# A state-space stage reordered on TensorE, VectorE and ScalarE

## The reference

```python
acs = cumsum(a)                                        # per chunk of 128 tokens
decay = exp(where(lower, acs_i - acs_j, -inf))
cb = einsum('cign,cjgn->cijg', Cm, Bm)
y = einsum('cijgh,cjghp->cighp', cb * decay, xdt)      # inside a chunk
states = einsum('cjgn,cjghp->cghpn', Bm, xdt * exp(acs_last - acs))
h_next = h * exp(acs_last) + states                    # across chunks
y += einsum('cign,cghpn->cighp', Cm, h_in) * exp(acs)
...
ssm = rms_norm((D * xs + y_forward + y_backward) * silu(z), gnorm_g)
```

## Time and profile before

| what | us |
|---|---|
| three runs | 1209.51, 1210.97, 1211.55 |
| their median | 1210.97 |
| the profiled execution | 1211.39 |
| span of its core | 1209.1 |
| busy: TensorE, VectorE, ScalarE | 1160.4, 698.0, 499.5 |
| mean granted clock of TensorE | 0.997 of 2.4 GHz |

### The profile page before, as it was taken

The page is one execution under the profiler, slowest core; times in us unless marked ns, Lnnn a source line. Parts: engine busy times, 40 slices in busy tenths (PEclk is TensorE's granted clock), DMA queues, the critical chain, the costliest instruction groups (busy, mean ns, idle before and its releaser), DMA issues.

```text
span 1209.1 us, 18264 instructions
## 1 busy us (share of the span) xinstructions
PE 1160.4 (96%) x7450; PEld 948.5 (78%) x7450; DVE 698.0 (58%) x1176; ACT 499.5 (41%) x756; POOL 8.5 (1%) x16
## 2 busy tenths in 40 slices
PE   4999999999999999999999999999889998999998
PEld 3777776687688888888887767898455897999998
DVE  3499998853542334423333378986769546456544
ACT  4343235652443332222222333366358635554442
POOL 0100000000000000000000000000000000000000
PEclk9999999999999999999999999999999999999999
DMA  9745345016553222333124563344021157546532
GB/s 358 257 140 202 138 157 202 1 62 218 180 168 105 87 73 84 130 113 104 50 73 143 192 210 105 106 138 140 1 93 48 53 180 256 176 146 215 194 116 93
DMA packets 121933, 166.49 MB, mean 138 GB/s; under 512 B 4509, under 2 KB 112391, under 8 KB 117639
## 3 DMA queue, kind: packets, MB, share of 16 engines
q1 hardware_dynamic: 121430, 164.99, 40.9%
q10 hardware_dynamic: 433, 0.51, 0.2%
HBM read 164.44 MB, written 1.05 MB: 137 GB/s over the span
## 4 chain that ended last, share of the span: by engine, by line
PE 75%; DVE 18%; ACT 4%; DMA 2%; issue 2%; SPq 0%; ACTq 0%; POOL 0%; DVEq 0%
PE acc L1929 20%; PE acc L1930 20%; PE acc L1931 20%; DVE Y L1258 6%; DVE w_lo L555 2%; PE acc L1991 1%; PE pmod L1868 1%; PE acc L1993 1%; PE acc L1992 1%; PE p L1816 1%; PE acc L1816 1%; DMA xin<-in_ctx 1%; DVE sm L1341 1%; PE acc L2562 1%; PE p L2149 1%
## 5 line engine op out<-in xcount | busy, mean ns | idle before, releaser
L555 DVE TENSOR_TENSOR w_lo<-raw,w_hi 128x1024 fp32r<-128x1024 f32 x234 | 259.0, 1148 | 247.7 <-ACT w_hi L545 247.3
L545 ACT ACTIVATE w_hi<-raw 128x1024 fp32r<-128x1024 f32 (+1 forms) x236 | 221.5, 987 | 436.3 <-PE acc L1931 407.0
L1929 PE MATMUL acc<-Hhi,w_hi 128*128 128x512 f32 (+1 forms) x976 | 334.4, 343 | 6.5 <-POOL ptap L627 4.5
L1930 PE MATMUL acc<-Hlo,w_hi 128*128 128x512 f32 (+1 forms) x976 | 331.7, 340 | 0.0
L1931 PE MATMUL acc<-Hhi,w_lo 128*128 128x512 f32 (+1 forms) x976 | 331.7, 340 | 0.0
L1929 PEld LDWEIGHTS acc<-Hhi,w_hi 128*128 128x128 f32 x976 | 185.9, 190 | 31.6 <-issue 8.5
L1931 PEld LDWEIGHTS acc<-Hhi,w_lo 128*128 128x128 f32 x976 | 185.8, 190 | 20.4
L1930 PEld LDWEIGHTS acc<-Hlo,w_hi 128*128 128x128 f32 x976 | 186.0, 191 | 19.8
L1929 PE MATMUL acc<-hid_hi,w_hi 128*128 128x512 f32 (+1 forms) x448 | 157.2, 351 | 0.0
L1930 PE MATMUL acc<-hid_lo,w_hi 128*128 128x512 f32 (+1 forms) x448 | 155.8, 348 | 0.0
L1931 PE MATMUL acc<-hid_hi,w_lo 128*128 128x512 f32 (+1 forms) x448 | 155.8, 348 | 0.0
(11 more groups left out here) (351 smaller groups left out, 1362.6 us busy)
## 6 DMA issues: line engine op xcount, KB each, us to landing
raw<-in_mod_w SPq DMA_DIRECT2D x48, 1024.0 KB, 5.3
raw<-in_ffn_w_in SPq DMA_DIRECT2D x44, 1024.0 KB, 5.1
raw<-in_od_w_in SPq DMA_DIRECT2D x15, 1024.0 KB, 5.3
raw<-in_ffn_w_out SPq DMA_DIRECT2D x16, 768.0 KB, 4.2
raw<-in_ev_w_in SPq DMA_DIRECT2D x10, 1024.0 KB, 7.5
raw<-in_ffn_w_out SPq DMA_DIRECT2D x16, 640.0 KB, 3.9
raw<-in_od_w_out SPq DMA_DIRECT2D x8, 1024.0 KB, 6.1
raw<-in_ev_w_out SPq DMA_DIRECT2D x8, 768.0 KB, 6.1
```

The source lines that it names most:

```text
L545: nc.scalar.activation(w_hi[:, w % 2, c0:c1], raw[:, r % RAW_SLOTS, c0:c1], ACT.Copy)\
L555: nc.vector.tensor_tensor(w_lo[:, w % 2, c0:c1], raw[:, r % RAW_SLOTS, c0:c1], w_hi[:, w % 2, c0:c1].bitcast(F32), ALU.subtract).then_inc( ...
L1929: mm(outs[m], hi[:, j, cols], xh, start=(first and j == 0), stop=False)
L1930: mm(outs[m], hi[:, j, cols], xl, start=False, stop=False)
```

## The change

TensorE: decays 0 and 1 go ahead of state products 0 to 2; the wait for `CB` moves behind products 3 and 4; decays 4 and 5 are issued after across 3, so that the decays run two steps ahead; each group b is `intra` twice, two decays, `inter`, two decays, and the sum of the group before, which also waits for `yg_ready` (its bank is the one that gating reads first). Modulation units 0 and 1 of the last group go ahead of the last sum, units 2 and 3 to the place where 0 and 1 were, and none is left in the pair loop's rounds; the first waits for decay 15 instead of the final root. VectorE: `masked(0)` behind `xw(2)`; `xw(4)` ahead of `join(1)`; `join` multiplies into `from_w`, ahead of its wait for the product, and adds from there; each chunk's addition right after its second `scaled`; both masked decays of a group ahead of the gating of the group before; the reciprocal of `qsc` ahead of the last gating. ScalarE: a dummy exponential first; decays 0 and 1 ahead of the state copies, two copies per state ahead of decays 2 and 3; squares after q = 9 and 13; the root of `qsc` after decay 15, then the squares of groups 2 and 3; the dummy root is gone.

```diff
@@ -971,14 +971,29 @@
                     f = 2 * (n - 12)
                     A(Z[:, f:f + 2, :], acc[:, lo:lo + 2, 0:LAT], ACT.Silu).then_inc(read_act, 1)
 
-            act.wait_ge(s("qsc_copied"), 1)
-            A(qsc[:, 0:LT, :], qsc[:, 0:LT, :], ACT.Sqrt, scale=1.0 / C_HD, bias=epsc[:, 0:1]).then_inc(s("qsc_root"), 1)
+            step(A(sm[:, 0, 7:8], epsc[:, 0:1], ACT.Exp))
             act.wait_ge(s("cb_mm"), 1)
             A(CB, pmod[:, :].rearrange("p (n i) -> p n i", n=4), ACT.Copy).then_inc(s("cb_ready"), 1)
-            for k in range(4):
-                act.wait_ge(s("xw_used"), (2, 2, 5, 5)[k])
-                A(state[:, k // 2 * 2, k % 2, :], acc[:, k % 2, :], ACT.Copy)\
-                    .then_inc(s("state_act"), 1)
+
+            def decay(q):
+
+                act.wait_ge(s("seg_mm"), q + 1)
+                if q >= 4:
+                    act.wait_ge(s("intra_mm"), q // 2 - 1)
+                A(seg[:, q % 4, :], RB(q), ACT.Exp).then_inc(s("decay_ready"), 1)
+
+            def state_copy(k):
+
+                act.wait_ge(s("xw_used"), 3 * k + 2)
+                for g in range(2):
+                    A(state[:, 2 * k, g, :], acc[:, g, :], ACT.Copy).then_inc(s("state_act"), 1)
+
+            decay(0)
+            decay(1)
+            state_copy(0)
+            state_copy(1)
+            decay(2)
+            decay(3)
 
             def square_y(b):
 
@@ -989,14 +1004,13 @@
                     A(ysq[:, f % 2, :], XC[:, f, 0:LAT], ACT.Square).then_inc(s("ysq_ready"), 1)
 
 
-            for q in range(16):
-                act.wait_ge(s("seg_mm"), q + 1)
-                if q >= 4:
-                    act.wait_ge(s("intra_mm"), q // 2 - 1)
-                A(seg[:, q % 4, :], RB(q), ACT.Exp).then_inc(s("decay_ready"), 1)
-                if q % 4 == 3 and q > 3:
-                    square_y(q // 4 - 1)
-            A(sm[:, 0, 7:8], epsc[:, 0:1], ACT.Sqrt)
+            for q in range(4, 16):
+                decay(q)
+                if q in (9, 13):
+                    square_y(q // 4 - 2)
+            act.wait_ge(s("qsc_copied"), 1)
+            A(qsc[:, 0:LT, :], qsc[:, 0:LT, :], ACT.Sqrt, scale=1.0 / C_HD, bias=epsc[:, 0:1]).then_inc(s("qsc_root"), 1)
+            square_y(2)
             square_y(3)
 
             act.wait_ge(s("ssy_mm"), KD)
@@ -1664,13 +1678,13 @@
             def join(k, used):
 
                 dve.wait_ge(s("state_act"), 2 * k)
-                dve.wait_ge(s("xw_used"), used)
-                to, frm = state[:, 2 * k - 1, :, :], state[:, 2 * k - 2, :, :]
-                step(V_.tensor_tensor(to.rearrange("p g (h n) -> p (g h) n", n=S_HD),
+                kept, frm = from_w[:, k - 1, :], state[:, 2 * k - 2, :, :]
+                step(V_.tensor_tensor(kept.rearrange("p (h n) -> p h n", n=S_HD),
                                       frm.rearrange("p g (h n) -> p (g h) n", n=S_HD),
                                       EX[:, 7 + k, :].unsqueeze(2).to_broadcast([P, S_HEADS, S_HD]), ALU.mult))
+                dve.wait_ge(s("xw_used"), used)
                 for g in range(2):
-                    ins = V_.tensor_tensor(state[:, 2 * k - 1, g, :], state[:, 2 * k - 1, g, :],
+                    ins = V_.tensor_tensor(state[:, 2 * k - 1, g, :], kept[:, g * 512:(g + 1) * 512],
                                            acc[:, 2 + g, :], ALU.add)
                 ins.then_inc(s("state_dve"), 1)
 
@@ -1693,24 +1707,25 @@
                                  CB[:, 2 * c + b // 2, :].unsqueeze(1).to_broadcast([P, 4, P]), ALU.mult)\
                     .then_inc(s("m_ready"), 1)
 
+            def both_ways(c, used):
+
+                dve.wait_ge(s("scaled_ready"), used)
+                V_.tensor_tensor(SCALED[c, 0], SCALED[c, 0], SCALED[c, 1], ALU.add).then_inc(s("across_ready"), 1)
+
             xw(2)
+            masked(0)
             xw(3)
+            xw(4)
             join(1, 3)
-            xw(4)
             xw(5)
-            masked(0)
             join(2, 6)
             scaled(0)
             scaled(1)
             masked(1)
             scaled(2)
+            both_ways(1, 3)
             scaled(3)
-            dve.wait_ge(s("scaled_ready"), 4)
-            for c in range(LT):
-                V_.tensor_tensor(SCALED[c, 0], SCALED[c, 0], SCALED[c, 1], ALU.add).then_inc(s("across_ready"), 1)
-            dve.wait_ge(s("qsc_root"), 2)
-            step(V_.reciprocal(qsc[:, 0:LT, :], qsc[:, 0:LT, :]))
-            step(V_.tensor_scalar(qsc[:, 0:LT, :], qsc[:, 0:LT, :], C_HD ** -0.5, None, ALU.mult))
+            both_ways(0, 4)
 
             def gate_y(b):
 
@@ -1722,12 +1737,16 @@
                                                  in1=acc[:, b, i * LAT:(i + 1) * LAT], op0=ALU.mult, op1=ALU.add))
                     V_.tensor_tensor(y, y, Z[:, f, :], ALU.mult).then_inc(s("yg_ready"), 1)
 
-            for k in range(8):
-                if k >= 2:
-                    masked(k)
-                if k % 2 == 0 and k:
-                    gate_y(k // 2 - 1)
-            gate_y(3)
+            for b in range(4):
+                if b < 3:
+                    masked(2 * b + 2)
+                    masked(2 * b + 3)
+                if b == 3:
+
+                    dve.wait_ge(s("qsc_root"), 2)
+                    step(V_.reciprocal(qsc[:, 0:LT, :], qsc[:, 0:LT, :]))
+                    step(V_.tensor_scalar(qsc[:, 0:LT, :], qsc[:, 0:LT, :], C_HD ** -0.5, None, ALU.mult))
+                gate_y(b)
 
             def gated_norm(p):
 
@@ -1854,7 +1873,7 @@
                 if k == 0 and n == 3:
                     pe.wait_ge(s("yn_ready"), BT)
                 if k == 0 and n == 5:
-                    pe.wait_ge(s("yrt_ready"), 1)
+                    pe.wait_ge(s("decay_ready"), 16)
                 if k == 4 and n == 5:
                     pe.wait_ge(s("mod_ready"), 6)
                 if n == 5:
@@ -2492,15 +2511,15 @@
                                  XW[:, n % 2, g * 512:(g + 1) * 512], start=bool(start), stop=bool(stop))
                     ins.then_inc(s("xw_used"), 1)
 
-            states(0, 3)
             pe.wait_ge(s("rows_ready"), 2)
             pe.wait_ge(s("maskB_ready"), 4)
-            pe.wait_ge(s("cb_ready"), 1)
             pe.wait_ge(s("xs_act"), 4)
             decays(0)
             decays(1)
+            states(0, 3)
             pe.wait_ge(s("state_act"), 2)
             states(3, 5)
+            pe.wait_ge(s("cb_ready"), 1)
             decays(2)
             decays(3)
             pe.wait_ge(s("state_dve"), 1)
@@ -2513,10 +2532,13 @@
             across(2)
             pe.wait_ge(s("scaled_ready"), 2)
             across(3)
+            decays(4)
+            decays(5)
             pe.wait_ge(s("scaled_ready"), 3)
 
             def sum_y(b):
 
+                pe.wait_ge(s("yg_ready"), 2 * b + 2)
                 for f in (2 * b, 2 * b + 1):
                     pe.wait_ge(s("ysq_ready"), f + 1)
                     for g in range(LT):
@@ -2524,18 +2546,18 @@
                                  start=(f == 0), stop=(f == KD - 1))
                     ins.then_inc(s("ssy_mm"), 1)
 
-            for k, (b, c) in enumerate(SEG):
+            def intra(k):
+
+                b, c = SEG[k]
                 pe.wait_ge(s("m_ready"), k + 1)
                 for h in range(4):
                     ins = mm(acc[64 * (h % 2):64 * (h % 2) + 64, b, h // 2 * LAT + c * P:h // 2 * LAT + (c + 1) * P],
                              XS[c][:, b, h * S_HD:(h + 1) * S_HD], seg[:, 2 * k % 4, h * P:(h + 1) * P],
                              start=(c == 0 and h < 2), stop=False, skip_group_check=True)
                 ins.then_inc(s("intra_mm"), 1)
-                for q in (2 * k + 4, 2 * k + 5):
-                    if q < 16:
-                        decays(q)
-                if c == 0:
-                    continue
+
+            def inter(b):
+
                 pe.wait_ge(s("across_ready"), 2)
                 for c_ in range(LT):
                     for i in range(2):
@@ -2543,8 +2565,21 @@
                                  SCALED[c_, 0][:, (2 * b + i) * P:(2 * b + i + 1) * P], cst("ident"), start=False,
                                  stop=(c_ == 1), skip_group_check=True)
                 ins.then_inc(s("inter_mm"), 1)
-                if k % 2 == 1 and k > 1:
-                    sum_y(k // 2 - 1)
+
+            for b in range(4):
+                intra(2 * b)
+                intra(2 * b + 1)
+                if b < 3:
+                    decays(4 * b + 6)
+                    decays(4 * b + 7)
+                inter(b)
+                if b < 2:
+                    decays(4 * b + 8)
+                    decays(4 * b + 9)
+                if b:
+                    sum_y(b - 1)
+            for k in (0, 1):
+                mod_unit(KD * 5 + k)
             sum_y(3)
 
 
@@ -2593,13 +2628,11 @@
             scores_pair(0)
             pe.wait_ge(s("yrt_ready"), 1)
             scores_pair(1)
-            for k in (0, 1):
```

(5 more changed lines are left out.)

## The result

The changed kernel takes 1200.43 us (median of 4, 1200.08 to 1201.26) against 1210.24 (median of 4, 1209.21 to 1211.55): a ratio of 0.9918, interval 0.9905 to 0.993. That is 9.8 us or 0.8% faster. In six more runs it had 1200.12.

The account below looks back on a forecast made before the run. The state-space stage was taken as bound by hand-overs between engines, no engine being full. Terms -2.95 - 4.1 + 0.35 - 1.4 = -8.1 us from a median of 1210.97 gave 1202.9, range 1200.5 to 1206.8.

Parts of the forecast that it names:

- the ScalarE loop would bind: Steady part: masked decays wait for exponentials, 4.8 instead of 1.2; only -4.5 in all, 1206.5 us; chance 0.14.
- an absorbed shift: Behind the pair loop: a load there swallows the whole gain, leaving 1211 us; chance 0.03.
- units are worth nothing: Pair loop: VectorE's stretch swallows all that moving the modulation units gives; -6.7 in all, 1204.3 us; chance 0.12.
- more is gained: Steady part and pair loop: waits of 1.8 vanish, units give 2.0; -10.5 in all, 1200.5 us; chance 0.1.
- The front: Stage entry to first `scaled`: reordered queues start `scaled(0)` near 859.5 instead of 862.46, -2.95 us.
- The steady part: First `scaled` to last gating's end: VectorE's work unchanged, waits of 5.94 replaced by 1.8, -4.1 us.
- new waits: VectorE's steady part: 0.6 before `scaled(1)`, 0.2, 0.7 and 0.3 before masked 5, 6 and 7, 1.8 us in all.
- The tail: Last gating to final root: two modulation units ahead of the last sum overrun the last square, +0.35 us.
- The pair loop: Score pairs up to the output projection: two modulation units taken out give 2.0, 0.6 given back, -1.4 us.
- The 0.6 given back: Pair loop, 914.35 to 928.47: nearly full VectorE limits the faster start, 0.6 us lost, between bounds 0 and 2.0.
- The clock: State-space stage: TensorE's waits drop its clock from 2.4 to 1.2 GHz, +33 us, 1244; chance 0.03.
- the forecast's own range: Whole kernel: 1201.3 to 1204.8 us, from bounds of tail, units and 0.1 for each moved operation; chance 0.58.

Follow-up runs that it names:

- units_back: Changed kernel with modulation units 0 and 1 back behind the second score pair, 2 and 3 back in the pair loop's rounds: 1202.80 us.
- before_again: The kernel before, measured and profiled again with no edit: 1211.83 us.
- masks_back: Changed kernel with VectorE's old order of masked decays and gatings, all else kept: 1205.79 us.
- before_fill: Kernel before plus six matmuls never read, four behind intra(6) and two ahead of the last sum, no order changed: 1208.47 us, ratio 0.9975.

## Why the prediction was right and where it was wrong

- **Direction and mechanism** were right. VectorE's wait for `inter` is gone, waits for ScalarE are 0.90 in all, and the projection starts 9.5 earlier. The rival that the ScalarE loop would bind has fallen (0.90, not 4.8), and so has the one of an absorbed shift: the stretch from the projection to the last output copy is 251.68 and 251.61. The rival that units are worth nothing fell with 1.41 in the loop. The measured time is that of the rival "more is gained" (1200.5), but its mechanism is not there: 1.39 of waits are left, and the units gave 1.41, not 2.0.
- **The front**, -2.95, measured -2.87. But I gave it all to the order. The runs divide it: 1.40 for the order (of which some 0.8 for the multiplication of `join` ahead of its wait) and 1.47 that stays when the order is undone, 1.43 of it at the place of the table load of 1.28. The walk had the load moved too, so the total came out; what it lacked was the split.
- **The steady part** is the first mis-sized term: -4.1 forecast, -4.75 measured. I counted 1.8 of new waits and took the small gaps as 0.86. Measured are 0.49 + 0.17 + 0.57 + 0.16 = 1.39, and 25.68 - 23.63 - 1.39 = 0.66. The loop that makes these waits passes through two `intra`, which I priced at 0.59 each from a place where other work follows each; back to back they cost 1.03 together. That this is why the waits are shorter is argued, not tested.
- **The tail** is the second: +0.35 forecast, -0.02 measured. The units end (884.93) before the last square (884.80 and 0.42, so 885.22). The 0.35 stands in the forecast without a working: gating 2 ends at 882.47, the units 2.46 later, the last square 2.75 later, so they end 0.29 before it and cost nothing. The measured -0.02 is no gain by itself (repeats give 0.96 and 0.97). But without the units the tail is longer by 0.24 and the third score pair late by 1.06 (units_back), since the clock falls; the forecast, which has the term below zero in no case, had no place for that.
- **The pair loop**: -1.4 forecast, -1.41 measured, and +1.41 when taken back. The 0.6 given back by VectorE's stretch is there too: the lead rises by 1.95 and then falls by some 0.5.
- **The clock** is the step that failed. The forecast has it as the only way to a slower kernel, says that this stage's pauses are too short for it, and so takes the 1210.97 of the kernel before as a time without falls: the clock's term in the sum is nothing. The profile it rested on showed 1.00; another profile of the same kernel shows 0.50 to 0.68 from 888 to 892, behind a wait as long (2.07 and 2.06). It is a cost of the kernel before, in some executions and not in others, which the change takes away. Between the quickest class of its runs (1209.4) and all of them (1210.24 in the first four, 1211.5 later) lie 0.8 to 2. The Trainium skill, TensorE: Matmul & The Clock Gate, section HAM oscillation, tells of waits for DMA behind which the array is throttled and the next work starts cold. This case's traces agree that the work behind a wait can start cold (before_again, units_back and masks_back), and have it behind waits of 1.45 to 2.07 us for another engine. I asked of one execution whether the change could bring a fall, and not whether it could take one away.

The account: 8.1 + 0.65 (steady part) + 0.37 (tail) - 0.08 (front) = 9.04, the profile's 9.05. The terms of the stage were thus off by 0.95 in all. With 9.05 taken from its base of 1210.97 the forecast would have said 1201.9, inside its range; 1200.43 is 1.5 less, and the range, whose lower end is 1210.97 - 10.5, had nothing set aside for that. From the quickest class, 1209.4 - 9.05 would be 1200.35. How the 1.5 divides stays open: the clocks of the three runs behind 1210.97 are not on record, the profiled one took 1211.39 with no fall in the stage and the latest entry of all, and against before_fill (1208.47), whose profile has no fall in the stage, the changed kernel (1200.12) gains 8.35, not 9.05. The upper end of the forecast's own range, 1204.8, does not follow from the bounds that it names either: 0.65 in the tail and 1.4 in the units alone give 1204.95.

## What to carry to other kernels

In a stage bound by hand-overs, list for each in-order engine what it still has to do while the other works, and put both pieces of such work ahead of the operation that waits; here undoing this one swap on VectorE cost 5.1 us, with its share of the clock, and undoing the producer's look-ahead 0.5. A wait of TensorE costs more than its length where the clock can fall behind it: look at several executions' mean clock and times before you trust one profile, and put independent matmuls into the wait. With matmuls that compute nothing the kernel before was 0.25% faster here, so an order that moves useful ones there can gain twice.

## What was not expected of the hardware

- The same program with a wait of 2.06 or 2.07 us at the same place was profiled once without and once with a fall of TensorE's clock to 1.2 GHz behind it; 48 of 65 executions had a mean below 0.997, and the times follow it (1209.4, 1211.6, 1213.8).
- At the lower level the eight records of `inter` took 2.08 instead of 1.11, and a score pair's four 2.08 instead of 1.13.
- One `intra` product by itself costs 0.59 to the start of the next work, two back to back 1.03 together.
